# Second mixing of a two-block transformer kernel: two z or gate rows between the two heads of each delta pair

## The chip, the cores and the metric

The kernel runs as one program on one core of a Trainium2 chip. The metric is the device time of one execution in microseconds (us), lower being better; medians over runs are compared. The engines are PE (matrix multiply), DVE (vector), ACT (activation functions), POOL and SP; the last two issue only DMAs in the part of the kernel that matters here. Each engine runs its own list of instructions in order, and semaphores make one wait for another.

## The reference

Two transformer blocks in a row on a sequence of 512 tokens of width 1024. The change lies in the second block, in its "mixing", where one input projection feeds a latent attention branch and a gated delta-rule branch:

```python
h = modulate(x, g_mix[l], sh2, sc2)
proj = h @ w_in[l]
q_lat, kv_lat, k_pe, gq, gk, gv, ga, gb, gz, gates = jnp.split(proj, split_at, axis=-1)
y_mla = mla_branch(q_lat, kv_lat, k_pe, ...) @ w_o_mla[l]
y_gdn = gated_deltanet_branch(jnp.concatenate([gq, gk, gv], axis=-1), ga, gb, gz, ...) @ w_o_gdn[l]
gate_mla, gate_gdn = jnp.split(jax.nn.sigmoid(gates), N_BRANCH, axis=-1)
mixed = (gate_mla * y_mla + gate_gdn * y_gdn) @ w_out[l]
```

In the delta branch each of 8 heads has q, k and v of 128 channels. They pass a causal convolution of width 4 and a silu; q and k are normed; then a lower triangular system of 64 by 64 is solved for every chunk of 64 tokens (here by doubling in six levels), before a recurrence over the eight chunks:

```python
qkv = jax.nn.silu(causal_depthwise_conv(qkv, w_conv))
q = l2norm(to_chunks(q, DK)) * (DK ** -0.5)
k = l2norm(to_chunks(k, DK))
A = jnp.where(strict, jnp.einsum('bhnid,bhnjd->bhnij', k_beta, k) * L, 0.0)
T = lax.linalg.triangular_solve(A + eye, jnp.broadcast_to(eye, A.shape), left_side=True, lower=True, unit_diagonal=True)
w = jnp.einsum('bhnij,bhnjd->bhnid', T, k_beta * jnp.exp(decay)[..., None])
u = jnp.einsum('bhnij,bhnje->bhnie', T, v * beta[..., None])
attn_intra = jnp.einsum('bhnid,bhnjd->bhnij', q, k) * L
```

## The kernel before

Stages follow each other on every engine. The one that matters is called `delta`. In it the projection `h @ w_in` is made row by row: a "row" is a block of 128 output channels for all 512 tokens. On PE a row is 24 matmuls (`pe_three`, L237 to L239; `mix2h_Hh` and `mix2h_Hl` are the high and low parts of the input, `Wh` and `Wl` those of the weights). There are 57 rows, in the order of the list `ROWS`: 24 rows "qkv" (head, and c = 1 for k, 0 for q, 2 for v), 2 rows "kl", 6 "ql", 1 "kp", 8 "z" and 16 "g". Row 0 is made before the stage. Row n lands in one of two PSUM banks.

What is done with a row depends on its kind. A qkv row is convolved on DVE (`conv_dve`, four instructions, L2393 and L2396), then silu and, for k and q, a square on ACT; its norm follows in the next two rows (`sum_at`: four small matmul pairs on PE at L2333, a root on ACT, a reciprocal and a diagonal matrix on DVE at L2417 and L2419; `bc_at`: one broadcast matmul at L2321 and the scaling on DVE at L2410). A z or g row costs ACT one silu or sigmoid into the small ring `SPL` (L2384), and POOL one DMA from it to DRAM (`rows_pool`); it costs DVE nothing. For each row ACT also makes `Wh` (L217) and DVE makes `Wl` (L229) of the next row's weights.

Into the rows the eight heads' own work is woven. `row_steps` counts passes n = 0, 1, 2, ...; all three engines follow the same count. A pass does on each engine first the row's part, then one step of each live head, the older head first (and on DVE and ACT last the convolution, or the silu or spill, of row n). At most `NCX` = 2 heads live at once, and a head may start only when its v row is behind:

```python
if todo and at_row["qkv", todo[0], 2] < n and len(live) < NCX:
    live.append(make_head(todo.pop(0)))
live = [g for g in live if next(g, "end") != "end"]
```

A head that starts in pass s does its step j in pass s + j, and the next one may come in pass s + 16. The steps that matter below (`head_pe`, `head_act`, `head_dve`; names are those of the semaphores' keys):

- Step 0: PE `ha` (L2470); DVE two additions (L2581, L2583); ACT exponentials (L2533 to L2541).
- Step 1: PE `hkk`, 16 matmuls (L2477, L2478). It waits for the norm of the head's q.
- Step 2: PE `hkt` and `hvt` (both L171), which wait for DVE's `hla` (L2589) and `han` (L2600) of the same pass.
- Step 3: PE `hyi` (L171), which waits for `hkd` on ACT (L2549), and that for `hkb` on DVE (L2605).
- Steps 4, 6, 8, 10, 12: PE `hm1` (L2505) and, from 6 on, `hxt` (L171); ACT copies the results out (L2562, L2565).
- Steps 5, 7, 9, 11, 13: PE `hm2` (L2516); DVE waits for it and subtracts (`hy`, L2617); in steps 3 to 11 DVE then masks for the next level (`ham`, L2613).
- Step 14: PE `hw` and `hu` (L2522, L2525), each copied out by ACT (L2569, L2571).

After the last row (56) PE has passes 57 and 58 without a row, then six short products `keys_pe` (L246) in passes 59 to 64, then what is left of the heads. The next stage, `state` (its first matmul is L2861), needs all heads.

Of the kernel before, what the change touches and what calls it, by code (L numbers as in the profile page):

```python
# [96 lines left out]
def build(nc, a, out, upto="end"):  # L97
# [10 lines left out]
    def slot(name):  # L108
        m = Marks(sem(name), 16)
        dmas.append(m)  # L110
        return m
# [45 lines left out]
    def ps(b, k=1):  # L157
        return ps_t[:, b, :] if k == 1 else ps_t[:, b:b + k, :].rearrange("p b t -> p (b t)")
# [22 lines left out]
    def weight(name, blk, n, kind):  # L181

        i = len(tiles)
        tiles.append((name, blk, n, kind))
        if kind == "split":
            split_of[i] = len(split_of)
        return i
# [22 lines left out]
    def w_hi(e, i):  # L210

        s = split_of[i]
        tile_of[s] = i
        w_landed(e, i)
        if s >= NS:
            PE.wait_ge(e, ("w", tile_of[s - NS]))
        A.then_inc(e.activation(w_parts(i)[0], w_raw(i), ACT.Copy), ("w_hi", i))  # L217
# [267 lines left out]
    class Early:  # L485
# [60 lines left out]
        def rows_act(self, e, norm):  # L546
            PE.wait_ge(e, (norm.tag, "rstd"))
            A.then_inc(e.activation(self.rb, norm.bank, ACT.Copy), (norm.tag, "rows"))
# [1352 lines left out]
    class FeedForward:  # L1901
# [192 lines left out]
        def x(self, e, nb):  # L2094
# [39 lines left out]
    NSP = 3  # L2134
    SPL = PH.t("spl", NSP * 512, k=NSP)
# [26 lines left out]
    spl_out = [slot(f"spl_out{i}") for i in range(NSP)]  # L2162
# [15 lines left out]
    PAIRS = [[("qkv", h, c) for h in (2 * i, 2 * i + 1) for c in (1, 0, 2)] for i in range(4)]  # L2178
    OTHER = [("kl", n, 0) for n in range(2)] + [("ql", n, 0) for n in range(6)] + [("kp", 0, 0)] \
        + [("z", n, 0) for n in range(8)] + [("g", n, 0) for n in (*range(8, 16), *range(8))]  # L2180
    ROWS = PAIRS[0] + OTHER[0:5] + PAIRS[1] + OTHER[5:13] + PAIRS[2] + OTHER[13:21] + PAIRS[3] + OTHER[21:33]
    at_row = {key: n for n, key in enumerate(ROWS)}
    spill = {key: n for n, key in enumerate(k for k in OTHER if k[0] not in ("kl", "kp"))}
    NLD = len(spill)
    LD = nc.dram_tensor("rows_dram", [NLD, 128, 512], F32, kind="Internal").ap()
    t_row = [weight("w_in_qkv", 3 * n + c, 1024, "split") if kind == "qkv" else weight("w_in_" + kind, n, 1024, "split")
             for kind, n, c in ROWS]
    t_uk = [weight("w_ukv_k", nb, 256, "plain") for nb in range(8)]
# [37 lines left out]
    def decay_act(e):  # L2226
        PE.wait_ge(e, "tcv")
        V.wait_ge(e, "tcv")
        pv = ps(4).rearrange("p (b s h) -> p b s h", b=4, s=16)
        A.then_inc(e.activation(tcv[:, :, 2, :], pv[:, :, 0, :], ACT.Exp))  # L2230
        A.then_inc(e.activation(tcv[:, :, 3, :], pv[:, :, 2, :], ACT.Exp), "tcv")
# [51 lines left out]
    def part(h, c):  # L2283
        return (QD, KDt, Ut)[c][:, h, :]
# [15 lines left out]

    NROW = len(ROWS)
    LAT = {"k": ("kl", 2), "q": ("ql", 6)}
# [6 lines left out]
    def rows_pe(e):  # L2309
        for n in range(NROW + 2):  # L2310
            if n < NROW:
                if n >= 2:
                    (V if ROWS[n - 2][0] == "qkv" else A).wait_ge(e, ("row_out", n - 2))
                if n:
# [27 lines left out]
    def rows_act(e):  # L2342
        for n in range(NROW + 2):
            if 1 < n < NROW - 1:
                w_hi(e, t_row[n + 1])
            if n == 2:
                decay_act(e)
            if n in sum_at:
                m = sum_at[n]
                r = R4[:, 4 * (m % 3):4 * (m % 3) + 4]  # L2350
                if m >= 3:
                    V.wait_ge(e, ("ndg", m - 3))
                PE.wait_ge(e, ("nsum", m))
                A.then_inc(e.activation(r, ps(6 + m % 2)[:, 0:4], ACT.Sqrt, bias=eps1), ("nr2", m))
            if n in LSUM:
                lat_root_act(e, LSUM[n])
            yield
            if n < NROW:
                kind, h, c = ROWS[n]
                if kind == "qkv":  # L2360
                    cv = part(h, c)
                    V.wait_ge(e, ("row_out", n))
                    A.then_inc(e.activation(cv, cv, ACT.Silu), ("silu", h, c))
                    if c != 2:
                        m = norm_of[n]
                        A.wait_ge(e, ("silu", h, c))
                        if c == 0:
                            PE.wait_ge(e, ("nsum", m - 1))
                        A.then_inc(e.activation(AN[:, h, :], cv, ACT.Square), ("nsq", m))
                elif kind in ("kl", "kp"):  # L2370
                    PE.wait_ge(e, ("row", n))
                    if kind == "kl":
                        lat_square_act(e, "k", h, ps(n % 2))
                    else:
                        PE.wait_ge(e, ("k", "lsum"))
                    A.then_inc(e.activation(KL[:, h, :] if kind == "kl" else KP, ps(n % 2), ACT.Copy), ("row_out", n))
                else:
                    s = spill[ROWS[n]]
                    PE.wait_ge(e, ("row", n))
                    if kind == "ql":  # L2380
                        lat_square_act(e, "q", h, ps(n % 2))
                    if s >= NSP:
                        spl_out[s % NSP].wait_ge(e, ("spl", s - NSP))
                    A.then_inc(e.activation(SPL[:, s % NSP, :], ps(n % 2),  # L2384
                                            {"z": ACT.Silu, "g": ACT.Sigmoid}.get(kind, ACT.Copy)), ("row_out", n))
            yield
# [43 lines left out]
            yield  # L2430

    def rows_pool(e):
        for s, key in enumerate(spill):
            A.wait_ge(e, ("row_out", at_row[key]))
            spl_out[s % NSP].then_inc(e.dma_start(LD[s], SPL[:, s % NSP, :]), ("spl", s))

    def spilled(e):
        for s in range(NLD - NSP, NLD):
            spl_out[s % NSP].wait_ge(e, ("spl", s))
# [184 lines left out]
    def delta_act(e):  # L2624
        x_out.wait_ge(e, "x")
        row_steps(chain(rows_act(e), keys_act(e)), lambda h: head_act(e, h))
# [6 lines left out]
    def lat_square_act(e, s, n, o):  # L2633

        if n > 1:
            V.wait_ge(e, (s, "lsq", n - 1))
        A.then_inc(e.activation(LSQ if n else LACC[s], o, ACT.Square), (s, "lsq", n))
# [20 lines left out]
    def lat_root_act(e, s):  # L2658
        PE.wait_ge(e, (s, "lsum"))
        A.then_inc(e.activation(LR[s], ps(6)[:, 0:4], ACT.Sqrt, bias=eps1, scale=1.0 / (128 * LAT[s][1])), (s, "lroot"))  # L2660
# [572 lines left out]
    def gpsimd(e):  # L3233
        for tag, stage in (("ada1", ada1_pool), ("swa", mix1_pool), ("wout1", wout1_pool), ("query", query_pool),
                           ("gates", gates_pool), ("dense", dense_pool), ("fin", None), ("ffn1", ff1.pool), ("mix2", None),
                           ("delta", rows_pool), ("state", state_pool), ("heads", br1.pool),
                           ("b2", b2_pool), ("wout2", None), ("ffn2", None)):
            if tag in on and stage:
                stage(e)
            G.mark(("end", tag))  # L3240
# [199 lines left out]
```

## Time and profile before

| what | value |
|---|---|
| median of 3 runs | 3385.17 us (3382.62 to 3386.49) |
| span of the profiled execution, first to last instruction | 3377.5 us |
| PE busy in that span | 3226.2 us, 96% |
| stage `delta` from row 1 on | 2054.0 us to the start of `state` at 2623.4 us |
| mean granted PE clock over the whole span | 0.978 |

The profiled execution gives its span, 3377.5 us; no other time of its own is recorded, and the runs' median lies 7.7 us above it. "Busy" of PE is the time in which matmuls are under way. The granted clock is a share of full speed. A row of the kind "L171 ... [2.42 <-DVE gdnh_c L2589]" says that the engine stood idle for 2.42 us before this instruction and that DVE's instruction at line 2589 released it.

### The profile page before, as it was taken

To read this page: it belongs to the slowest core of one execution; us is meant where nothing else is said; L and a number is where in the kernel's file an instruction comes from. 1 tells how busy PE (TensorE), PEld (TensorE's weight loads), DVE (VectorE), ACT (ScalarE), POOL (GpSimd) and SP (SyncE) were. 2 spreads that over 40 slices of the span, in tenths; PEclk is the share of its full clock that TensorE was granted. 3 is DMA by queue.
4 is the path that set the end of the run, shared out by engine and by line. 5 is a ranking of instruction groups with operands and counts; after the bars stand their busy time and mean duration, and the time that the engine had idled before them with its cause. 6 is when DMAs were issued, how large, how long until landed. Compare 5 with 4: busy or idle time off the path is not lost.

```text
span 3377.5 us, 40568 instructions
## 1 busy us (share of the span) xinstructions
PE 3226.2 (96%) x16035; PEld 2671.0 (79%) x16035; DVE 2063.3 (61%) x3549; ACT 1330.8 (39%) x2340; POOL 621.1 (18%) x588
## 2 busy tenths in 40 slices
PE   8999999999999999999799997899998999999998
PEld 5764899998888888888688885687787667778887
DVE  5766887876888888888765525455443445443333
ACT  3131238983444444444422225454444124232322
POOL 0001349971222222222200000000000000000000
PEclk9999999999999999999999998899999999999999
DMA  7326244569999999998255522121221222223222
GB/s 259 125 82 222 90 137 164 201 236 349 333 332 331 331 337 327 337 328 307 80 181 183 175 88 94 53 75 62 92 80 39 70 91 72 94 81 99 95 95 80
DMA packets 190062, 574.48 MB, mean 170 GB/s; under 512 B 16305, under 2 KB 81969, under 8 KB 171569
## 3 DMA queue, kind: packets, MB, share of 16 engines
q1 hardware_dynamic: 152000, 368.06, 32.0%
q0 software_dynamic: 37872, 203.84, 16.8%
q8 instruction: 127, 2.08, 0.3%
q14 instruction: 63, 0.51, 0.0%
HBM read 523.99 MB, written 47.84 MB: 169 GB/s over the span
## 4 chain that ended last, share of the span: by engine, by line
PE 85%; DVE 8%; ACT 4%; DMA 2%; issue 1%; POOL 1%; SPq 0%; DVEq 0%; ACTq 0%; POOLq 0%
PE ps L237 11%; PE ps L238 11%; PE ps L239 11%; PE ps L1774 5%; PE ps L1773 5%; PE ps L1772 5%; PE ps L1524 4%; PE ps L1526 4%; PE ps L1525 4%; PE ps L246 4%; PE ps L744 2%; PE ps L171 1%; PE ps L1650 1%; PE ps L747 1%; DMA hidden_dram<-peerg_HS 1%; PE ps L2516 1%
## 5 line engine op out<-in xcount | busy, mean ns | idle before, releaser
L229 DVE TENSOR_TENSOR Wl<-W,Wh 128x1024 fp32r<-128x1024 f32 (+1 forms) x336 | 408.8, 1217 | 660.0 <-ACT Wh L217 659.8
L217 ACT ACTIVATE Wh<-W 128x1024 fp32r<-128x1024 f32 x362 | 377.3, 1043 | 540.7 <-PE ps L239 505.3
L1524 PE MATMUL ps<-peer_Hh,Wh 128*128 128x384 f32 x1024 | 347.8, 340 | 3.0 <-DVE Wl L229 1.4
L1526 PE MATMUL ps<-peer_Hh,Wl 128*128 128x384 f32 x1024 | 344.1, 336 | 0.0
L1525 PE MATMUL ps<-peer_Hl,Wh 128*128 128x384 f32 x1024 | 343.6, 336 | 0.0
L1737 POOL DMA_INDIRECT peerv_UV<-peer_uv,peer_EX x128 | 209.6, 1637 | 638.5 <-DVE peer_Y L1811 583.4
L1772 PE MATMUL ps<-peerv_VH,peer_HTh 128*128 128x512 f32 x768 | 300.8, 392 | 11.1 <-DVE peer_HTl L1838 11.1
L1774 PE MATMUL ps<-peerv_VH,peer_HTl 128*128 128x512 f32 x768 | 301.8, 393 | 0.0
L1773 PE MATMUL ps<-peerv_VL,peer_HTh 128*128 128x512 f32 x768 | 301.5, 393 | 0.0
L237 PE MATMUL ps<-f_Hh,Wh 128*128 128x512 f32 x656 | 257.1, 392 | 5.7 <-DVE Wl L229 5.7
L238 PE MATMUL ps<-f_Hl,Wh 128*128 128x512 f32 x656 | 256.3, 391 | 0.0
L239 PE MATMUL ps<-f_Hh,Wl 128*128 128x512 f32 x656 | 256.3, 391 | 0.0
L237 PE MATMUL ps<-mix2h_Hh,Wh 128*128 128x512 f32 x512 | 212.3, 415 | 12.6 <-DVE Wl L229 6.3
L238 PE MATMUL ps<-mix2h_Hl,Wh 128*128 128x512 f32 x512 | 206.4, 403 | 0.0
L239 PE MATMUL ps<-mix2h_Hh,Wl 128*128 128x512 f32 x512 | 206.3, 403 | 0.0
L1524 PEld LDWEIGHTS ps<-peer_Hh,Wh 128*128 128x128 f32 x1024 | 193.0, 188 | 8.5 <-ACT peerg_HS L1539 2.7
L1525 PEld LDWEIGHTS ps<-peer_Hl,Wh 128*128 128x128 f32 x1024 | 193.0, 189 | 2.8
L1526 PEld LDWEIGHTS ps<-peer_Hh,Wl 128*128 128x128 f32 x1024 | 192.7, 188 | 0.0
L1702 DVE TENSOR_TENSOR peerv_VL<-peerv_VR,peerv_VH 128x1024 fp32r<-128x1024 f32 x128 | 160.1, 1251 | 47.9 <-ACT peerv_VH L1698 47.2
L1772 PEld LDWEIGHTS ps<-peerv_VH,peer_HTh 128*128 128x128 f32 x768 | 145.1, 189 | 43.7 <-DVE peer_HTl L1838 13.0
L1774 PEld LDWEIGHTS ps<-peerv_VH,peer_HTl 128*128 128x128 f32 x768 | 144.8, 189 | 30.6
L1773 PEld LDWEIGHTS ps<-peerv_VL,peer_HTh 128*128 128x128 f32 x768 | 145.0, 189 | 27.5
(545 smaller groups left out, 6550.2 us busy)
## 6 DMA issues: line engine op xcount, KB each, us to landing
W<-peer_u SPq DMA_DIRECT2D x128, 512.0 KB, 6.8
peerv_VR<-peer_v SPq DMA_DIRECT2D x128, 512.0 KB, 5.2
gates_dram<-peerg_GB SPq DMA_DIRECT2D x12, 2048.0 KB, 7.3
peerv_GR<-gates_dram SPq DMA_DIRECT2D x32, 768.0 KB, 8.2
f_AW<-w_ada POOLq DMA_DIRECT2D x48, 512.0 KB, 4.4
W<-w_gate SPq DMA_DIRECT2D x44, 512.0 KB, 3.3
W<-w_up SPq DMA_DIRECT2D x44, 512.0 KB, 3.4
swa_AW<-w_ada POOLq DMA_DIRECT2D x32, 512.0 KB, 4.5
```

The source lines that it names most:

```text
L217: A.then_inc(e.activation(w_parts(i)[0], w_raw(i), ACT.Copy), ("w_hi", i))
L229: (G if i in lo_on_pool else V).then_inc(e.tensor_tensor(lo, w_raw(i), hi.bitcast(F32), SUB), ("w", i))
L237: e.matmul(o[0:m, :], hi[:, j, :], rhs[0][:, k, :], start=k == 0, stop=False)
L238: e.matmul(o[0:m, :], hi[:, j, :], rhs[1][:, k, :], start=False, stop=False)
L239: ins = e.matmul(o[0:m, :], lo[:, j, :], rhs[0][:, k, :], start=False, stop=k == nk - 1)
L1524: e.matmul(o, hi[:, k, :], H2[0][:, k, 0:TD], start=k == 0, stop=False)
L1525: e.matmul(o, hi[:, k, :], H2[1][:, k, 0:TD], start=False, stop=False)
L1526: ins = e.matmul(o, lo[:, k, :], H2[0][:, k, 0:TD], start=False, stop=k == 7)
L1737: uv_in[k % NUV].then_inc(e.indirect_dma_start(UV[:, k % NUV, :], None, a["peer_uv"], bass.IndirectOffsetOnAxis(ap=EX[:, k:k + 1], axis=0) ...
L1772: e.matmul(o, HTh[:, s, sl], VH[:, s, d], start=n == 0, stop=False)
L1773: e.matmul(o, HTh[:, s, sl], VL[:, s, d], start=False, stop=False)
L1774: ins = e.matmul(o, HTl[:, s, sl], VH[:, s, d], start=False, stop=n == 127)
```

## The change

The list `ROWS` is put in another order. Within each pair of heads, two z or g rows now stand between the three rows of the first head and the three of the second; these rows are taken from the runs behind the pairs, which shrink, so that later rows keep almost their place. The number and kind of rows stay. Because z and g rows now come in another order than in DRAM, the ring `SPL` gets its own numbering, `ring`, while the place in DRAM stays that of `spill`.

```diff
-    ROWS = PAIRS[0] + OTHER[0:5] + PAIRS[1] + OTHER[5:13] + PAIRS[2] + OTHER[13:21] + PAIRS[3] + OTHER[21:33]
+    KLS, QLS, KPS, ZS, GS_ = OTHER[0:2], OTHER[2:8], OTHER[8:9], OTHER[9:17], OTHER[17:33]
+
+    def apart(i, between):
+        return PAIRS[i][0:3] + between + PAIRS[i][3:6]
+
+    ROWS = apart(0, ZS[0:2]) + KLS + QLS[0:3] + apart(1, ZS[2:4]) + QLS[3:6] + KPS + ZS[4:5] + apart(2, ZS[5:7]) \
+        + ZS[7:8] + GS_[0:5] + apart(3, GS_[5:7]) + GS_[7:16]
     at_row = {key: n for n, key in enumerate(ROWS)}
     spill = {key: n for n, key in enumerate(k for k in OTHER if k[0] not in ("kl", "kp"))}
+    ring = {key: n for n, key in enumerate(k for k in ROWS if k in spill)}
...
-                    s = spill[ROWS[n]]
+                    s = ring[ROWS[n]]
...
     def rows_pool(e):
-        for s, key in enumerate(spill):
+        for key, s in ring.items():
             A.wait_ge(e, ("row_out", at_row[key]))
-            spl_out[s % NSP].then_inc(e.dma_start(LD[s], SPL[:, s % NSP, :]), ("spl", s))
+            spl_out[s % NSP].then_inc(e.dma_start(LD[spill[key]], SPL[:, s % NSP, :]), ("spl", s))
```

The rule of `row_steps` turns the order into the passes in which heads start:

| head | 0 | 1 | 2 | 3 | 4 | 5 | 6 | 7 |
|---|---|---|---|---|---|---|---|---|
| place of its v row, before | 2 | 5 | 13 | 16 | 27 | 30 | 41 | 44 |
| place of its v row, now | 2 | 7 | 15 | 20 | 28 | 33 | 42 | 47 |
| starts in pass, before | 3 | 6 | 19 | 22 | 35 | 38 | 51 | 54 |
| starts in pass, now | 3 | 8 | 19 | 24 | 35 | 40 | 51 | 56 |

What this does to an engine's list is seen at two places. The first is DVE in pass 53, where head 6 does its step 2 (`gdnh_c0_*` are the tiles of an even head, `gdnh_c1_*` those of an odd one). Before:

```order
L229 TENSOR_TENSOR Wl<-W,Wh 128x1024 [waits act_done] x2
L2589 SCALAR_TENSOR_TENSOR gdnh_c0_1<-ps,gdn_tc,gdnh_c0_1 128x128 [waits pe_done]
L2589 SCALAR_TENSOR_TENSOR gdnh_c0_1<-ps,gdn_tc,gdnh_c0_1 128x128 x3
L2593 TENSOR_TENSOR gdnh_c0_2<-gdnh_c0_1,consts_sb 128x512 [waits dve_done]
L2595 TENSOR_TENSOR gdnh_c0_3<-consts_sb,gdnh_c0_2 128x512 [waits dve_done]
L2598 TENSOR_TENSOR gdnq_QD<-gdnq_QD,gdnh_c0_0 128x512
L2600 TENSOR_TENSOR gdnc_AN<-ps,gdnc_AN 128x512
```

The same place with the change (lines are eight further down):

```order
L229 TENSOR_TENSOR Wl<-W,Wh 128x1024 [waits act_done] x2
L2625 TENSOR_TENSOR gdnh_c1_4<-gdnh_c1_4,ps 128x512 [waits pe_done]
L2597 SCALAR_TENSOR_TENSOR gdnh_c0_1<-ps,gdn_tc,gdnh_c0_1 128x128 x4
L2601 TENSOR_TENSOR gdnh_c0_2<-gdnh_c0_1,consts_sb 128x512 [waits dve_done]
L2603 TENSOR_TENSOR gdnh_c0_3<-consts_sb,gdnh_c0_2 128x512 [waits dve_done]
L2606 TENSOR_TENSOR gdnq_QD<-gdnq_QD,gdnh_c0_0 128x512
L2608 TENSOR_TENSOR gdnc_AN<-ps,gdnc_AN 128x512
```

Head 5's step 13, `hy` of the last level, which waits for a product of PE in this pass, now stands in front of head 6's step 2. It is the same in pass 21 (heads 1 and 2) and 37 (heads 3 and 4). Before, the odd head had nothing left to do in these passes.

The second place is DVE in passes 4 and 5, where head 0 does its steps 1 and 2. Before:

```order
L2396 SCALAR_TENSOR_TENSOR gdnq_QD<-ps,vecs_sb,gdnq_QD 128x509 [waits dve_done]
L229 TENSOR_TENSOR Wl<-W,Wh 128x1024 [waits act_done]
L2410 SCALAR_TENSOR_TENSOR gdnc_KD<-gdnc_KD,ps 128x512 [waits pe_done]
L2417 RECIPROCAL small<-small 128x4 [waits act_done]
L2419 TENSOR_TENSOR DG<-consts_sb,small 128x512 [waits dve_done]
L2589 SCALAR_TENSOR_TENSOR gdnh_c0_1<-ps,gdn_tc,gdnh_c0_1 128x128 x4
```

And now:

```order
L2418 SCALAR_TENSOR_TENSOR gdnq_QD<-gdnq_QD,ps 128x512 [waits pe_done]
L229 TENSOR_TENSOR Wl<-W,Wh 128x1024 [waits act_done]
L2597 SCALAR_TENSOR_TENSOR gdnh_c0_1<-ps,gdn_tc,gdnh_c0_1 128x128 [waits pe_done]
L2597 SCALAR_TENSOR_TENSOR gdnh_c0_1<-ps,gdn_tc,gdnh_c0_1 128x128 x3
L2601 TENSOR_TENSOR gdnh_c0_2<-gdnh_c0_1,consts_sb 128x512 [waits dve_done]
```

The convolution of head 1's q row and the norm work of head 1's k row no longer stand between head 0's steps; rows 3 and 4 are z rows now.

The third place is ACT in pass 54, head 6's step 3. Before:

```order
L217 ACTIVATE Wh<-W 128x1024 [waits w_in0]
L2549 ACTIVATE gdnc_KD<-ps,gdn_tc 128x128 [waits dve_done,pe_done]
L2549 ACTIVATE gdnc_KD<-ps,gdn_tc 128x128 x3
L2553 ACTIVATE X<-ps,gdn_tc 128x128 [waits pe_done]
L2553 ACTIVATE X<-ps,gdn_tc 128x128 x3
```

And now:

```order
L217 ACTIVATE Wh<-W 128x1024 [waits w_in0]
L2577 ACTIVATE mix2_YG<-ps 128x512 [waits pe_done]
L2579 ACTIVATE X<-ps 128x512 [waits pe_done]
L2557 ACTIVATE gdnc_KD<-ps,gdn_tc 128x128 [waits dve_done]
L2557 ACTIVATE gdnc_KD<-ps,gdn_tc 128x128 x3
```

The two copies of head 5's step 14, which wait for PE's `hw` and `hu` behind this pass's row, have come in front of `hkd`; before, they lay one or more passes earlier.

## Rows read from the trace of the kernel before

**Rows 1.** The page: the span, and PE's busy time in it

```profile
span 3377.5 us, 40568 instructions
PE 3226.2 (96%) x16035; PEld 2671.0 (79%) x16035; DVE 2063.3 (61%) x3549; ACT 1330.8 (39%) x2340; POOL 621.1 (18%) x588
```

**Rows 2.** Windows: rows 1 to 56; behind them. Length, busy times, clock, DMA

```profile
2054.00:2572.00 518.00, 474.76 (x2446) 393.78 (x2447) 258.55 (x387) 254.58 (x421) 15.69 (x29) 0.94 0.22 75
2572.00:2623.00 51.00, 40.20 (x251) 32.85 (x249) 18.55 (x33) 17.87 (x36) 2.06 (x3) 0.90 0.09 26
```

**Rows 3.** PE's waits from 2054 to 2624: total, times, longest

```profile
PE ps L171 <- DVE gdnh_c L2589: 13.7, 6, 2.5
PE ps L171 <- ACT gdnc_KD L2549: 11.4, 5, 3.3
PE ps L171 <- DVE gdnc_AN L2600: 11.3, 6, 2.0
```

**Rows 4.** Timeline of PE, passes 24 and 25: hm2, hkt, hvt; hyi

```profile
2292.62 1.05 PE L2516 MATMUL ps<-gdnh_c,gdnh_c 128*128 128x128 f32 x8
2296.09 0.87 PE L171 MATMUL ps<-consts_sb,gdnc_KD 128*128 128x128 f32 x4 [2.42 <-DVE gdnh_c L2589]
2298.75 1.12 PE L171 MATMUL ps<-consts_sb,X 128*128 128x128 f32 x4 [1.79 <-DVE gdnc_AN L2600]
...
2310.07 0.66 PE L171 MATMUL ps<-consts_sb,gdnh_c 128*128 128x128 f32 x4 [1.77 <-ACT gdnc_KD L2549]
```

**Rows 5.** Timeline of DVE, pass 24: hy, ham, hla, the last is han

```profile
2293.71 0.69 DVE L2617 TENSOR_TENSOR gdnh_c<-gdnh_c,ps 128x512 f32<-128x512 f32 x1 [4.87 <-PE ps L2516]
2294.32 0.68 DVE L2613 TENSOR_TENSOR gdnh_c<-gdnh_c,consts_sb 128x512 f32<-128x512 f32 x1
2294.92 1.12 DVE L2589 SCALAR_TENSOR_TENSOR gdnh_c<-ps,gdn_tc,gdnh_c 128x128 f32<-128x128 f32 x4
...
2298.01 0.68 DVE L2600 TENSOR_TENSOR gdnc_AN<-ps,gdnc_AN 128x512 f32<-128x512 f32 x1
```

**Rows 6.** Timeline of ACT, pass 25: the older head's copy, hkd

```profile
2308.39 0.59 ACT L2565 ACTIVATE gdnh_c<-ps 128x512 f32<-128x512 f32 x1
2308.87 1.14 ACT L2549 ACTIVATE gdnc_KD<-ps,gdn_tc 128x128 f32<-128x128 f32 x4
```

**Rows 7.** Timeline of PE, passes 53 and 54: hkt, hvt; hyi

```profile
2549.17 0.60 PE L171 MATMUL ps<-consts_sb,gdnc_KD 128*128 128x128 f32 x4
2549.60 0.60 PE L171 MATMUL ps<-consts_sb,X 128*128 128x128 f32 x4
...
2555.50 0.60 PE L171 MATMUL ps<-consts_sb,gdnh_c 128*128 128x128 f32 x4
```

**Rows 8.** Windows over rows 25, 42 and 54 alone, columns as in rows 2

```profile
2299.50:2306.80 7.30, 7.30 (x26) 5.89 (x25) 1.61 (x5) 0.00 (x0) 0.00 (x0) 0.74 0.22 72
2452.50:2459.70 7.20, 7.20 (x27) 5.76 (x26) 5.13 (x7) 3.46 (x6) 0.00 (x0) 0.76 0.00 0
2549.90:2555.40 5.50, 5.50 (x27) 4.59 (x26) 2.50 (x5) 2.87 (x10) 0.54 (x1) 1.00 0.19 73
```

**Rows 9.** Timeline of PE, head 0 in passes 4, 5, 5 and 6

```profile
2094.78 1.05 PE L2333 MATMUL ps<-consts_sb,gdnc_AN 128*128 128x1 f32 x8 [0.74 <-ACT gdnc_AN L2369]
...
2110.68 0.66 PE L171 MATMUL ps<-consts_sb,gdnc_KD 128*128 128x128 f32 x4 [2.33 <-DVE gdnh_c L2589]
2113.34 1.12 PE L171 MATMUL ps<-consts_sb,X 128*128 128x128 f32 x4 [2.00 <-DVE gdnc_AN L2600]
...
2126.21 1.11 PE L171 MATMUL ps<-consts_sb,gdnh_c 128*128 128x128 f32 x4 [3.29 <-ACT gdnc_KD L2549]
```

**Rows 10.** Timeline of PE, head 7 alone at the stage's end

```profile
2612.49 1.06 PE L2516 MATMUL ps<-gdnh_c,gdnh_c 128*128 128x128 f32 x8
2614.93 1.16 PE L2505 MATMUL ps<-gdnh_c,gdnh_c 128*128 128x128 f32 x8 [1.38 <-DVE gdnh_c L2613]
...
2617.36 1.13 PE L2516 MATMUL ps<-gdnh_c,gdnh_c 128*128 128x128 f32 x8 [0.83 <-ACT gdnh_c L2565]
```

More of the change, by code:

```diff
@@ L2180, in build @@
         + [("z", n, 0) for n in range(8)] + [("g", n, 0) for n in (*range(8, 16), *range(8))]
-    ROWS = PAIRS[0] + OTHER[0:5] + PAIRS[1] + OTHER[5:13] + PAIRS[2] + OTHER[13:21] + PAIRS[3] + OTHER[21:33]
+    KLS, QLS, KPS, ZS, GS_ = OTHER[0:2], OTHER[2:8], OTHER[8:9], OTHER[9:17], OTHER[17:33]
[3 more added lines that the diff above has]
+        + ZS[7:8] + GS_[0:5] + apart(3, GS_[5:7]) + GS_[7:16]
+    assert sorted(ROWS) == sorted(sum(PAIRS, []) + OTHER)
     at_row = {key: n for n, key in enumerate(ROWS)}
     spill = {key: n for n, key in enumerate(k for k in OTHER if k[0] not in ("kl", "kp"))}
+    ring = {key: n for n, key in enumerate(k for k in ROWS if k in spill)}
     NLD = len(spill)
```

## Prediction

> **What bounds the kernel now.** I read the page first. PE is busy in 3226.2 of 3377.5 us [rows 1]; what can move is its idle time and the time in which its clock is low. The change touches only the stage with the 57 rows, so I took windows of that stretch next. From row 1 to the end of row 56 PE is busy in 474.8 of 518 us, so it idles for 43 us; behind the rows it idles for 10.8 of 51 us. DVE and ACT are half idle there (259 and 255 us) and DMA is at 0.22 [rows 2], so no engine but PE is full, and PE's idle time comes from chains between engines, not from load. The waits of PE in that stretch name the chains: `hkt` for DVE's `hla` 13.7 us in 6 waits, `hvt` for `han` 11.3 us in 6, `hyi` for ACT's `hkd` 11.4 us in 5 [rows 3]. All three belong to steps 2 and 3 of a head. Six waits for eight heads: the timeline shows that head 4 and head 6 have none. In pass 53 head 6's `hkt` and `hvt` follow the row at once, and so does its `hyi` in pass 54 [rows 7].
>
> **Why some heads wait.** Pass 24 has a z row behind it and no convolution in front; yet head 3 waits 2.42 and 1.79 us [rows 4]. DVE shows why: it stood 4.87 us until PE's `hm2` of head 2, which is in its step 5, then made `hy` and `ham`, and only then `hla` (at 2294.92) and `han` (at 2298.01) [rows 5]. DVE takes the older head first and waits in that step for a product that PE makes behind this pass's row, while PE comes to the younger head's `hkt` right behind that product. So the rule is: when a head does step 2 while an older one does an odd step from 5 to 13, PE waits for the whole DVE chain. In pass 25 the like happens on ACT: its copy of head 2's `hxt` (2308.39) comes before `hkd` (2308.87), and PE waits 1.77 us [rows 4, 6]. Head 6 has no older head at work, and DVE did `hla` under the row.
>
> **What the change does to these meetings.** Before, an odd head meets the even one in its step 5 (offset 3), now in its step 7 (offset 5). Both are odd: the wait stays. But the next even head now meets the odd one before it in that one's step 13 instead of its empty step 15, and its `hyi` stands behind that one's `hw` and `hu`. That gives waits to heads 4 and 6, which had none. I price it head by head; PE's own work and the count of instructions stay the same.
>
> *Heads 4 and 6* (passes 37, 38 and 53, 54). Step 13 has `hy` but no `ham`, so `hkt` waits 2.42 less 0.6, 1.8 us; `hvt` waits 1.79 to 2.0, I take 1.9; `hyi` behind two ACT copies instead of one with its last matmul just before: 1.8 [rows 4, 6, 9]. Then the clock: row 25, behind such a wait, took 7.3 us at a granted 0.74, row 54 took 5.5 at 1.00 [rows 8]; 0.74 is a mix of the two levels 1.2 and 2.4 GHz. So each pair of waits costs 1.8 us more in the next row. Row 42, behind a `hyi` wait, took 7.2 [rows 8], but not each such wait does this, so for the second row I take 0.5 of a possible 1.7. Last, `ham` of step 11 now delays step 0's additions by 0.6, and with them ACT's weights; 0.6, from 0 to 1.2. Together 1.8 + 1.9 + 1.8 + 1.8 + 0.5 + 0.6 = 8.4 per head, 16.8 us (from 2 x 5.5 with no clock term at all to 2 x 10).
>
> *Head 2* (passes 21, 22) gets the same 7.8, but has waits already: from 13.7 and 11.3 us the five heads 0, 1, 3, 5, 7 take about 12.1 and 9.8 at the prices in [rows 4, 9], which leaves 1.6 and 1.5 for head 2, and 1.3 of clock in proportion. 7.8 - 4.4 = 3.4. Its step 0 now falls among its own pair's rows: ACT's exponentials delay the square of q, as in pass 4, where PE waited 0.74 [rows 9]; 1.0, from 0 to 2. Together +4.4.
>
> *Head 0* gains. In pass 5 there is no older head; it waits 2.33 and 2.00 because the norm of head 1's k row and the convolution stand before `hla` [rows 9]. Rows 3 and 4 are z rows now and DVE has nothing there: -4.3. The 0.74 wait in pass 4 goes: -0.7. In pass 6 `hyi` waited 3.29 [rows 9]; now the convolution of row 5, the root and the diagonal come before `hkb`: +0.7 (from 0 to 1.5). One slow row fewer: -1.7. Together -6.0 (from -9 to -4).
>
> *Heads 1, 3, 5*: offsets of the same kind, waits as before. Head 1: 0. Head 3 now has its steps 2 and 3 beside its successors' k and q rows (26, 27), so `hkb` stands behind a norm: +1.6 (0 to 3). Head 5's step 0 falls on row 40, a k row, whose square then comes late: +1.6 (0 to 3). Together +3.2.
>
> *The end.* Head 7 starts in pass 56 instead of 54. Two of its steps, one level of `hm1` and `hm2`, leave the six passes with `keys_pe` and are done alone: there PE waits 1.38 and 0.83 [rows 10], +2.2. Its `hkk` in pass 57 has no row any more that covers the two additions on DVE (0.6 to 0.7 each, as their kind in [rows 5]) and ACT's first exponential behind them; PE's `hm1` and `hxt` of head 6, 1.7 us, stand in between, so I take +1.1 (an estimate, 0 to 3). Together +3.3 (2 to 5).
>
> Sum: -6.0 + 4.4 + 16.8 + 3.2 + 3.3 = +21.7. The profiled execution gives 3377.5 + 21.7 = 3399.2 us of span; the median of the runs lies 7.7 above the span, 3385.2 + 21.7 = **3407 us**.
>
> The clock terms in this sum are worth about 5 us. The Trainium skill ("TensorE: Matmul & The Clock Gate", Part 1: The HAM clock gate) says "For modeling, the ramp penalty is <1% of a typical kernel span"; by that one would leave them out, and the sum would be +17, 3402 us. I keep them, since rows 25 and 42 have their price beside them.
>
> The DMAs of the ring are as many as before and its three places are still used in the order of the rows; POOL issues nothing else then. I price that at nothing; if a spill came late, ACT would stand with the weights behind it. DMA at 0.22 [rows 2] speaks against it.
>
> **Rivals.** What a run of this kernel can tell from no change is about 0.2%, 6.8 us.
>
> 1. *The waits come as priced*: +12 to +32, centre +21.7. Chance 0.68.
> 2. *Heavier* (0.10): late DVE and ACT work in passes 20 to 27 and 36 to 43 carries on from pass to pass, so that the upper ends hold together: -4 + 5.4 + 20 + 6 + 5 = +32, 3418 us and above, up to +42. Against it: of PE's 43 us of idle time in the passes with rows, the three chains of steps 2 and 3 make 30 (36.4 less some 6 behind row 56) [rows 2, 3]; late weights are no large part of it.
> 3. *Absorbed* (0.15): the third meeting is cheaper. Step 13's `hy` alone costs 0.6 on DVE; if DVE could do part of head 6's step 2 beside it, or PE came later, only the `hyi` waits would stay: 2 x 2.3 + 1.5 - 6 + 3.3 = +3, 3388 us. For it speaks head 0's gain of 6, which is certain in kind; against it the order of DVE, in which `hy` stands ahead of `hla`. 0.10 of this within 0.2%, 0.05 slower.
> 4. *Faster* (0.07): the mechanism is DVE's convolutions and norms, not the meeting. Then thinning the qkv rows takes from heads 1, 3, 5 and 7 what it takes from head 0: with 6.0 at head 0 and a third of it at three others, -12, 3373 us. It decides if the four later pairs of waits drop by over 5 us each more than heads 4 and 6 gain. Against it: head 3 waits 2.42 and 1.79 with no convolution before it [rows 4, 5], as much as head 0 with one.
>
> **How the numbers follow.** Slower by over 0.2%: 0.68 + 0.10 + 0.05 = 0.83; within 0.2%: 0.10; faster 0.07. The range leaves out the fast case, most of the absorbed one and the top of the heavier one: 3390 to 3420. The likeliest case alone spans 3397 to 3417.
>
> **What would show it.** Right: PE's waits for `hla` and `han` (now L2597 and L2608) come in 7 waits each, sums near 15 and 14 us; those for `hkd` (L2557) in 8, near 18; passes 37 and 53 show about 3.7 us, where there was none; pass 5 shows none; behind the last `keys_pe` two levels stand alone; rows 38 and 54 take over 7 us at a clock near 0.75. Wrong: `hkt` of heads 4 and 6 without a wait, or the waits of heads 1, 3, 5 much under 4 us, would overturn the meeting rule; a stage longer by the sum with a kernel no slower would mean that the next stage took it back.

## The result and the profile after

The changed kernel takes 3399.93 us in the median of 4 runs (3397.92 to 3407.07), the kernel before on the same chip 3384.05 us; the ratio is 1.0055 with a 95% interval of 1.0043 to 1.0067, so it is slower by 0.55%. The profiled execution has a span of 3397.6 us against 3377.5. Of these 20.1 us, 17.5 lie in the stage with the rows (from row 1's first matmul to the first of `state`: 2057.0 to 2643.9 us, before 2054.0 to 2623.4). The other 3.0 lie ahead of the stage, where nothing was changed: in the traces of this case row 1 starts anywhere from 2054.0 to 2062.0 us. The rest behind the stage is the same within 0.4 us. I therefore compare stages. A stage length comes from one profiled execution; in all the runs below it and the medians agree within 3.4 us on the distance to the kernel before. Here the medians differ by 15.9 us: the profiled execution of the kernel before was one of its faster ones.

The page of the changed kernel, and windows over rows 1 to 55, over row 56 and over what lies behind it, to be read beside [rows 1, 2], where row 56 is in the first window:

```profile
span 3397.6 us, 40563 instructions
PE 3229.9 (95%) x16035; PEld 2671.2 (79%) x16035; DVE 2063.6 (61%) x3549; ACT 1331.3 (39%) x2340; POOL 621.8 (18%) x588
...
2057.00:2577.00 520.00, 465.26 (x2401) 386.06 (x2401) 257.20 (x385) 247.93 (x405) 15.15 (x28) 0.95 0.21 74
2577.00:2582.40 5.40, 5.40 (x27) 4.46 (x26) 0.00 (x0) 2.37 (x3) 0.54 (x1) 1.00 0.12 49
2582.60:2643.00 60.40, 44.24 (x271) 33.96 (x269) 19.22 (x35) 22.24 (x47) 2.06 (x3) 0.92 0.07 22
```

The instructions are the same. In the stage PE is busy for 514.9 us, before 515.0; it idles for 54.7 us beside the rows where it was 43.2, and for 16.2 behind them where it was 10.8. PE's waits in the stage (engine and line, who released it, total us, times, longest) answer to [rows 3]:

```profile
PE ps L171 <- ACT gdnc_KD L2557: 17.2, 8, 3.7
PE ps L171 <- DVE gdnh_c L2597: 15.2, 7, 2.5
PE ps L171 <- DVE gdnc_AN L2608: 13.5, 7, 2.0
PE ps L2524 <- ACT gdnh_c L2573: 5.2, 3, 3.5
```

The waits for `hla` (L2597) went from 13.7 us in 6 to 15.2 in 7, those for `han` (L2608) from 11.3 in 6 to 13.5 in 7, those for `hkd` (L2557) from 11.4 in 5 to 17.2 in 8. The fourth row is new: `hm2` waits for ACT's copies, before 0.8 us in one.

Passes 53 and 54 are where head 6 had no wait [rows 7]. The timeline of PE there now: `hm2` of head 5, `hkt`, `hvt`; `hw` of head 5; `hyi`:

```profile
2553.54 1.05 PE L2524 MATMUL ps<-gdnh_c,gdnh_c 128*128 128x128 f32 x8
2556.41 0.66 PE L171 MATMUL ps<-consts_sb,gdnc_KD 128*128 128x128 f32 x4 [1.82 <-DVE gdnh_c L2597]
2559.06 1.12 PE L171 MATMUL ps<-consts_sb,X 128*128 128x128 f32 x4 [2.00 <-DVE gdnc_AN L2608]
...
2566.53 1.05 PE L2530 MATMUL ps<-gdnh_c,mix_YG 128*128 128x128 f32 x8
...
2570.19 0.66 PE L171 MATMUL ps<-consts_sb,gdnh_c 128*128 128x128 f32 x4 [1.72 <-ACT gdnc_KD L2557]
```

DVE in pass 53 of the same kernel:

```profile
2554.63 0.69 DVE L2625 TENSOR_TENSOR gdnh_c<-gdnh_c,ps 128x512 f32<-128x512 f32 x1 [4.40 <-PE ps L2524]
2555.24 1.12 DVE L2597 SCALAR_TENSOR_TENSOR gdnh_c<-ps,gdn_tc,gdnh_c 128x128 f32<-128x128 f32 x4
...
2558.32 0.68 DVE L2608 TENSOR_TENSOR gdnc_AN<-ps,gdnc_AN 128x512 f32<-128x512 f32 x1
```

And ACT in pass 54, the copy of `hu` and then `hkd`:

```profile
2568.51 0.60 ACT L2579 ACTIVATE X<-ps 128x512 f32<-128x512 f32 x1 [0.29 <-PE ps L2533]
2569.00 1.14 ACT L2557 ACTIVATE gdnc_KD<-ps,gdn_tc 128x128 f32<-128x128 f32 x4
```

DVE stood idle for 4.40 us with all that head 6's step 2 needs at hand, because head 5's subtraction is ahead in its list and waits for PE. PE finishes that product and then waits 1.82 and 2.00 us for what DVE could have done meanwhile. Pass 37 with head 4 shows the same 1.8 and 2.0.

Head 0's gain, in passes 5 and 6 (`hkt`, `hvt`; `hyi`), against [rows 9]:

```profile
2107.15 0.60 PE L171 MATMUL ps<-consts_sb,gdnc_KD 128*128 128x128 f32 x4
2107.59 0.60 PE L171 MATMUL ps<-consts_sb,X 128*128 128x128 f32 x4
...
2118.18 0.83 PE L171 MATMUL ps<-consts_sb,gdnh_c 128*128 128x128 f32 x4 [3.74 <-ACT gdnc_KD L2557]
```

The clock, in windows over rows 38, 54 and 55 alone:

```profile
2409.50:2416.20 6.70, 6.70 (x26) 5.49 (x25) 1.57 (x5) 0.00 (x0) 0.00 (x0) 0.81 0.22 78
2559.80:2566.50 6.70, 6.70 (x26) 5.47 (x25) 1.62 (x5) 0.00 (x0) 0.00 (x0) 0.82 0.06 20
2570.60:2576.20 5.60, 5.60 (x28) 4.61 (x27) 2.51 (x3) 2.01 (x5) 0.54 (x1) 1.00 0.21 73
```

The row behind the two waits runs at 0.81 and costs 1.1 us more than 5.6; the row behind the `hyi` wait of 1.7 us is at full clock.

### The profile page after: what moved, and what is told of

The parts are those of the page before. It is cut to its first block, busy times and chain, and to the rows that moved or that the text cites. A ratio compares the mean times of both kernels' runs of the same rounds, so it can differ in the third digit from the quotient of the medians.

```text
span 3397.6 us, 40563 instructions
## 1 busy us (share of the span) xinstructions
PE 3229.9 (95%) x16035; PEld 2671.2 (79%) x16035; DVE 2063.6 (61%) x3549; ACT 1331.3 (39%) x2340; POOL 621.8 (18%) x588
## 4 chain that ended last, share of the span: by engine, by line
PE 80%; DVE 8%; ACT 5%; DMA 3%; POOL 2%; issue 1%; SPq 0%; DVEq 0%; ACTq 0%; POOLq 0%
PE ps L237 11%; PE ps L239 11%; PE ps L238 11%; PE ps L1773 5%; PE ps L1774 5%; PE ps L1772 5%; PE ps L1524 4%; PE ps L1526 4%; PE ps L1525 4%; PE ps L744 2%; PE ps L246 2%; DMA hidden_dram<-peerg_HS 1%; PE ps L171 1%; DMA adaw_AW<-w_ada 1%; PE ps L747 1%; PE ps L2524 1%
```

## The experiments

The runs are numbered by their paragraphs. My theory: what the change costs comes from which steps of two heads fall into one pass, given that DVE and ACT serve the older head first; the order of the rows sets this only through the starts. The rival: the convolutions and norms beside the heads, that is DVE's own load. All times are compared with the kernel before on the same chip; "stage" is from row 1 to `state` in the profile (569.4 before, 586.9 with the change).

**1. The starts alone** (rows as before).

```diff
+    START = [3, 8, 19, 24, 35, 40, 51, 56]
-            if todo and at_row["qkv", todo[0], 2] < n and len(live) < NCX:
+            if todo and at_row["qkv", todo[0], 2] < n and START[todo[0]] <= n and len(live) < NCX:
```

> The rows stand in the order of the kernel before; only the passes in which heads 1, 3, 5 and 7 may start are held back by two, to 8, 24, 40 and 56, as the change has them. Theory (meetings of steps decide): all waits of the change come, and head 0's gain does not, since rows 3 and 4 are qkv rows again; waits of PE for hla and han in 8 and 8, for hkd in 8; 3384 plus 20 to 26, about 3407 us. Rival (the place of the convolutions decides): the starts alone do nothing beyond the two lone steps at the end, 3384 to 3390 us.

Measured: 3405.39 us against 3382.04, ratio 1.0067 (1.0054 to 1.0081); stage 593.3, +23.9 us. PE's waits:

```profile
PE ps L171 <- DVE gdnh_c L2591: 18.0, 8, 2.8
PE ps L171 <- ACT gdnc_KD L2551: 16.6, 8, 3.3
PE ps L171 <- DVE gdnc_AN L2602: 14.6, 8, 2.0
```

No row has moved, and the whole loss is there, and more: eight waits of each kind, since head 0 keeps its own. The 6.4 us between the two stages, 23.9 and 17.5, are what the new row order itself gives. The rival's first form, by which the starts alone would do nothing beyond the end, is out.

**2. Head 7 alone held back to pass 56** (rows as before, with the condition of run 1), to price the end.

```diff
+    START = [0, 0, 0, 0, 0, 0, 0, 56]
```

> The kernel before with head 7 alone held back to pass 56; all other heads start as before. It isolates the term of the end, which the prediction put at 3.3 us. What the changed kernel's waits behind row 56 say (15.0 us against 9.1, less 0.6 before it) is about 5.3: 3382 plus 5, 3387 us, waits of PE behind the last row near 15 us with one of 3.5 on ACT's copy. If the prediction's size was right: 3385. Rival (the end costs nothing, all of the change lies in the passes with rows): 3382.

Measured: 3389.08 us against 3382.73, ratio 1.0022 (1.0013 to 1.0031); stage 575.6, +6.3 us. PE's waits behind row 56:

```profile
PE ps L2518 <- ACT gdnh_c L2567: 5.2, 3, 3.5
PE ps L2507 <- DVE gdnh_c L2615: 2.8, 2, 1.4
```

The end costs 6.3, not 3.3. In the changed kernel the same wait of 3.5 stands in pass 58. ACT of the changed kernel, timeline behind row 56: head 7's exponentials, a table load, the spill of row 56, and only then the copies of head 6; and PE's `hm2` that waits for them:

```profile
2586.93 1.26 ACT L2545 ACTIVATE gdnh_c<-gdnh_c,gdn_tc 128x128 f32<-128x128 f32 x4
2588.10 1.26 ACT L2549 ACTIVATE gdnc_AN<-gdnc_AN,gdn_nds 128x128 f32<-128x128 f32 x4
2589.38 1.28 ACT L2392 ACT_TABLE_LOAD   x1
2590.68 0.60 ACT L2392 ACTIVATE gdnh_spl<-ps 128x512 f32<-128x512 f32 x1
2591.17 0.59 ACT L2570 ACTIVATE gdnh_c<-ps 128x512 f32<-128x512 f32 x1
2591.65 0.60 ACT L2573 ACTIVATE gdnh_c<-ps 128x512 f32<-128x512 f32 x1
...
2592.40 1.52 PE L2524 MATMUL ps<-gdnh_c,gdnh_c 128*128 128x128 f32 x8 [3.51 <-ACT gdnh_c L2573]
```

In the passes with rows PE has a row's 5.6 us to cover step 0's work on ACT; here it has none.

**3. An offset of 4** (rows as before, with the condition of run 1).

```diff
+    START = [3, 7, 19, 23, 35, 39, 51, 55]
```

> Rows in the order of the kernel before; the odd heads may start one pass later than before (7, 23, 39, 55), an offset of 4. Theory: an odd head's step 2 now meets the older one's step 6, which asks nothing of DVE, so the waits for hla and han of heads 1, 3, 5 and 7 go (about -17.7 us); its step 3 meets step 7, so hyi waits some 4 us instead of 1.7 to 2.3 (+8); the next even head meets step 14 in its step 2 and nothing in step 3, no wait; one lone step more at the end, +1 to +3. Sum about -7, 3377 us (3370 to 3384). Rival (a later start costs by how much later it is): between before and the change, 3388 to 3396 us.

Measured: 3382.67 us against 3382.04, ratio 1.0 (0.9991 to 1.0009); stage 569.1. The time is inside the expected range, but the gain of 7 us did not come.

```profile
PE ps L171 <- ACT gdnc_KD L2551: 19.4, 5, 4.3
PE ps L171 <- DVE gdnc_AN L2602: 9.9, 5, 2.0
...
PE ps L171 <- DVE gdnh_c L2591: 4.1, 3, 2.3
```

The waits for `hla` fell from 13.7 to 4.1 as the theory says, and `hyi` paid 3.9 to 4.3 at each odd head. But five waits for `han` stayed: that of head 0 in pass 5, which was there before; one in pass 57, where no row stands between `hkk` and step 2; and three that stand behind norm work on DVE, in pass 21 (latent sum) and in passes 9 (latent sum) and 41 (norm of a q row), where `hla` too waits 0.9. Those three are no meeting. The rival has a share after all: without a meeting, a norm beside step 2 costs PE 3 us.

**4. One row between the heads of each pair** instead of two; the same starts as run 3.

```diff
-    ROWS = apart(0, ZS[0:2]) + KLS + QLS[0:3] + apart(1, ZS[2:4]) + QLS[3:6] + KPS + ZS[4:5] + apart(2, ZS[5:7]) \
-        + ZS[7:8] + GS_[0:5] + apart(3, GS_[5:7]) + GS_[7:16]
+    ROWS = apart(0, ZS[0:1]) + KLS + QLS[0:3] + ZS[1:2] + apart(1, ZS[2:3]) + QLS[3:6] + KPS + ZS[3:5] + apart(2, ZS[5:6]) \
+        + ZS[6:8] + GS_[0:5] + apart(3, GS_[5:6]) + GS_[6:16]
```

> One z or g row between the heads of a pair instead of two, the other rows moved to keep the later pairs' places. The starts are 3, 7, 19, 23, 35, 39, 51, 55. Theory: as the offset of 4 with the old rows, and part of head 0's gain besides (its convolution in pass 4 goes, the norm in pass 5 stays): 3368 to 3382 us, about 3375. Rival (thinning is what it takes, more rows between are better or worse in proportion): half way between before and the change, about 3392 us.

Measured: 3369.81 us against 3382.04, ratio 0.9966 (0.9954 to 0.9978); stage 556.1. The size fits, one reason given for it does not: head 0 still waits 2.3 and 2.0 in pass 5, since row 4 is a k row there and its norm stands ahead of `hla`. What is gone against run 3 are the waits in pass 9 and pass 21, three waits for `han` being left of five. Against the change itself, with its two rows, this is 31 us of stage: one row fewer turns a loss into a gain.

**5. One row between in pair 0 alone**, pairs 1 to 3 together; the starts of runs 3 and 4. The edit takes the place of the two added lines of run 4.

```diff
+    ROWS = apart(0, ZS[0:1]) + KLS + QLS[0:3] + PAIRS[1] + QLS[3:6] + KPS + ZS[1:5] + PAIRS[2] + ZS[5:8] + GS_[0:5] + PAIRS[3] \
+        + GS_[5:16]
```

> One row between the heads of pair 0 alone; the six rows of pairs 1, 2 and 3 stand together as before, one place later for pair 1. Starts as with one row everywhere (3, 7, 19, 23, 35, 39, 51, 55). Theory: what differs between the two runs of offset 4 (12 us) is where single norm sums and the latent sums fall, not the spread of convolutions: two of the passes with a head's step 2 (9 and 21) come free of them here too; 3370 to 3378 us. Rival (spreading each pair's convolutions is what gains): near the offset of 4 with the old rows, 3380 to 3384.

Measured: 3372.68 us against 3380.77, ratio 0.9976 (0.9965 to 0.9988); stage 562.9, half way between runs 3 and 4 (569.1 and 556.1). The waits for `han` are the same three of 6.0 us as in run 4, those for `hkd` 22.4 us in 6 against 19.4 in 5. So of the 13.0 us of stage between runs 3 and 4, 6.2 are where single sums fall and 6.8 the spread of the later pairs; by the medians, each against its own kernel before, it is 8.7 and 4.1. Both readings had a part, and these runs do not fix the shares more closely.

**6. DVE serves the younger head first in its step 2** (the changed kernel, rows as changed).

```diff
-    def row_steps(rows, make_head):
+    def row_steps(rows, make_head, first=()):
...
             if todo and at_row["qkv", todo[0], 2] < n and len(live) < NCX:
-                live.append(make_head(todo.pop(0)))
-            live = [g for g in live if next(g, "end") != "end"]
+                live.append([make_head(todo.pop(0)), -1])
+            for g in live:
+                g[1] += 1
+            over = [g for g in sorted(live, key=lambda g: g[1] not in first) if next(g[0], "end") == "end"]
+            live = [g for g in live if g not in over]
...
-        row_steps(rows_dve(e), lambda h: head_dve(e, h))
+        row_steps(rows_dve(e), lambda h: head_dve(e, h), (2,))
```

The second entry of `g` counts the head's steps; a head whose step is in `first` is served ahead of the other.

> The changed kernel; on DVE alone the head that is in its step 2 comes before the older head in that pass (every other pass as it was). Theory: hla and han no longer stand behind a subtraction that waits for PE; the waits of PE for them, 15.2 and 13.5 us in 7 each, fall under 8 us together, while those for hkd stay near 17 us; with the slow rows behind them -20 to -30, 3370 to 3380 us. Rival (DVE is late by its own load, convolutions and norms): the waits only move to the older head's next product, less than 8 us are gained.

Measured: 3364.32 us against 3382.04, ratio 0.9955 (0.9941 to 0.9968); stage 555.1, 31.8 us less than with the change and 14.3 less than before. The time lies below the expected 3370 to 3380; the waits came as expected.

```profile
PE ps L171 <- ACT gdnc_KD L2560: 18.0, 8, 3.7
...
PE ps L171 <- DVE gdnc_AN L2611: 4.0, 2, 2.0
...
PE ps L171 <- DVE gdnh_c L2600: 2.3, 2, 1.3
```

This is the direct test: the same instructions and starts, one order exchanged, and 28.7 us of waits for `hla` and `han` become 6.3. The four that remain lie in passes 21 and 42, beside norm work.

**7. The same, and ACT serves the younger head first in its step 3.**

```diff
-        row_steps(chain(rows_act(e), keys_act(e)), lambda h: head_act(e, h))
+        row_steps(chain(rows_act(e), keys_act(e)), lambda h: head_act(e, h), (3,))
```

> The changed kernel; as the run before, DVE takes the head in its step 2 first, and besides ACT takes the head in its step 3 first. Theory: hkd no longer stands behind ACT's copies of the older head; the waits of PE for hkd fall from 17 to about 8 us (head 0's 3.7 and those that hang on norms stay), -10 to -16 with the slow rows against the run with DVE alone: 3364 minus 12, 3352 us (3346 to 3358). Rival: ACT's place is not what holds hyi, but hkb on DVE: no change against 3364.

Measured: 3362.35 us against 3380.77, ratio 0.9942 (0.9926 to 0.9959); stage 549.2, 5.9 us less than run 6. The medians show less of it: 18.4 us below the kernel before, where run 6 was 17.7 below, with intervals that overlap (the profiled execution of run 6 is 3 us shorter behind the stage than the others). That this step shortened the time is thus seen in the waits and the stage of one trace each, not in the runs' times.

```profile
PE ps L171 <- ACT gdnc_KD L2560: 11.5, 5, 3.7
```

The waits in passes 22, 38 and 54, the ones that the change had made, are gone. Of the expected 10 to 16 us at least half did not come: the waits of heads 0, 1, 3 and 5 (3.8, 2.3, 3.1 and 2.0 us) stayed as they were in run 6, so they do not hang on ACT's copies; `hkb` or a norm ahead of it is what is left.

**8. Both orders on the kernel before** (the edits of runs 6 and 7).

> The kernel before with the same two orders of heads. Theory: the change costs 18 us only through the meetings, so with both orders free of them the two row orders come near each other; what is left between them is head 0 (6 to 7 us for the change) against the two lone steps at the end (5 us against it): 3352 plus or minus 4. Rival (the row order itself costs): before stays about 18 us ahead of the changed one, near 3335.

Measured: 3360.23 us against 3380.77, ratio 0.9933 (0.9916 to 0.995); stage 547.3. The absolute time was missed by 8 us for the reason given under run 7, but the question was the distance: 17.5 us of stage between the two row orders have become 1.9 (549.2 and 547.3). The medians of runs 7 and 8 are 2.1 us apart. With the meetings made harmless, two rows between or none hardly matters.

**9. One row between (the rows of run 4), younger first on DVE in steps 2 and 3, on ACT in step 3.**

```diff
+        row_steps(rows_dve(e), lambda h: head_dve(e, h), (2, 3))
+        row_steps(chain(rows_act(e), keys_act(e)), lambda h: head_act(e, h), (3,))
```

> One row between the heads of a pair, and younger first: DVE in steps 2 and 3, ACT in step 3. Theory: at offset 4 the odd heads wait 3.9 us in step 3 because DVE's subtraction and mask for the older head, which wait for PE, come before hkb; with hkb first, four waits of 3.9 us shrink to under 1: -14 to -22 against 3370, 3352 us (3346 to 3358). Rival: hy of the younger head, which now waits for hyi before the older head is served, gives the time back: 3365 to 3372.

Measured: 3362.77 us against 3380.77, ratio 0.9945 (0.9929 to 0.9962); stage 549.1, 7.0 less than run 4, half of what I expected. The waits for `hkd` went from 19.4 us in 5 to 9.9 in 4. Together with runs 7 and 8 this puts three row orders within 1.9 us of stage; what is left in all of them are head 0's and head 5's norm waits, the start of the stage and the end. Runs 6 to 9 beat both kernels; among 7, 8 and 9 there is no difference that these runs can tell.

## Why the prediction was right

The time was 3399.93 us where 3407 was forecast, inside the range. The kernel is slower, as forecast; by how much, 15.9 us between the medians and 17.5 of stage, is less than the 21.7 of the sum.

*The rule of meetings* held to the count: 7, 7 and 8 waits were forecast for `hla`, `han` and `hkd` with sums near 15, 14 and 18 us; 15.2, 13.5 and 17.2 came. Runs 1 and 6 show that it is the cause and not a companion.

*Heads 4 and 6*: 8.4 each was forecast. Waits of 1.8, 2.0 and 1.7 came (1.8, 1.9 and 1.8 forecast); the slow row cost 1.1 instead of 1.8 and there was no second one; late weights cost 0.2 instead of 0.6. Together 6.8 each. One of the signs named did not come: rows 38 and 54 took 6.7 us at 0.81 and 0.82, not over 7 near 0.75. But this count leaves out the short products of the same passes, some of which also ran at the low clock. From the start of row 36 to that of row 39, and from 52 to 55, the changed kernel takes 31.7 us where 22.5 stood before; about 1.0 of these 9.2 is the odd head's work that has moved there, net of what has left (an estimate from passes at full clock). That makes 8.2 each: the clock cost about what I had put down for it, in other places.

*Head 2*: +4.4 forecast. Its waits are 0.9, 1.8, 2.0 and 1.7 where there were 3.1, and the slow row 1.6 for 1.4; +3.5, or +3.3 counted with the short products in the same way.

*Head 0*: -6.0 forecast, -6.5 from the waits and rows of passes 4 to 7. With the short products, which before ran at the low clock behind these waits, the gain is larger. From the start of row 1 to that of row 8 the changed kernel takes 71.3 us where 84.9 stood before; about 3.8 of these 13.6 is work that has moved behind row 8 (again an estimate from passes at full clock), which leaves -9.8. Run 1, with the same starts and the old rows, takes 80.5, of which 0.9 is such work: 8.3 for the row order alone up to there. Its 6.4 for the whole stage is a balance of this gain and some loss later. The 0.74 wait of pass 4 did not vanish, it moved: PE waited 2.8 instead of 1.8 for the next thing, the norm of q.

*Heads 1, 3, 5*: 0, +1.6, +1.6 forecast; 0, -0.2, +1.3 came. Head 5's 1.7 us in pass 41 is as described. Head 3's `hyi` waited 2.3 where it waited 1.8 before, a third of the 1.6, and it lost the 0.6 for late weights that it had before row 24.

*The end*: +3.3 forecast, +6.3 measured by itself in run 2. The lone level is there, its 1.38 and 0.83 a second time. What I missed is ACT behind `hkk`: I priced the first exponential, and the copies of the older head also stand behind the rest of them, a table load and the last spill. The step's range, 2 to 5, was too short.

In the order of the heads and then the end, the parts give -9.8 + 0 + 3.3 - 0.2 + 8.2 + 1.3 + 8.2 + 6.3 = +17.3 for a stage that grew by 17.5. The sum of 21.7 was 4 too high. Its largest errors are head 0's gain, 4 too small, and the end, 3 too cheap; they have opposite signs, so that part of the closeness is luck. Head 3 was 1.8 too dear and head 2 about 1. The sentence on the clock rule of the Trainium skill ("TensorE: Matmul & The Clock Gate", Part 1) gave +17, and its sum fits better here. By the sum's own terms it gives nearer +18: the clock terms are 2.3 at each of heads 4 and 6, 1.0 net at head 2 and -1.7 at head 0, 3.9 together. But not because slow rows cost nothing: behind such waits each costs 1.1 to 2.4 us in the trace. The change made new ones (rows 38, 54) and took away others (rows 5 and 6 in pair 0, the second one at head 5), so that over the rows it is even within 1 us.

The 7.7 us that I put between the span and the runs' median is not a fixed part around the span: the changed kernel's profiled execution took 3399.42 us for a span of 3397.6, which is 1.8. The rest was that the profiled execution of the kernel before was a fast one.

Rival 2 (heavier) had one of its signs, the end above its bound, and not the others. Rival 3 (absorbed) is out by the waits of passes 37 and 53 and by run 1. Rival 4 (DVE's load) is out as the main cause by runs 1 and 6, but runs 3 and 6 show that it has its own passes, 9 and 41 in the one, 21 and 42 in the other, of about 3 us each. The prediction's head 0 was such a case; besides it I had norm work in the sum only at heads 3 and 5, and there as a delay of 1.6 us.

## What to carry to other kernels

Where two chains are woven into one another pass by pass on engines that work in order, list for each pass which step of one meets which step of the other, and look for a step that waits for a product of this very pass standing ahead of one that has all it needs. Putting the ready one first costs no instruction and on DVE alone was worth 32 us of stage here. On the kernel before, doing so on both engines gained 22.1 us of stage, the best order of rows tried 13.3. A change of spacing should be judged by the offsets it makes (3 to 5 kept the bad meeting and added another; 4 avoided both and paid with longer waits for `hyi`), and a start that moves toward the end of a stage by the work that used to cover it, on every engine.

## What the runs showed of the hardware

How long a slow row is after the same kind of wait varies: after `hkt` and `hvt` waits of 1.8 and 2.0 us, row 38 took 6.7 us at a clock of 0.81 and row 22 took 7.2 at 0.76; behind `hyi` waits of 1.7 rows 39 and 55 took 5.6, at 1.00. A single wait of 3.7 us (pass 6) gave a row of 7.1. An ACT table load shows 1.28 us, and the next activation starts 0.02 us behind its end (2589.38 plus 1.28, then 2590.68); the Trainium skill ("ScalarE: Activation LUTs", What ACT_TABLE_LOAD costs) agrees on the 1.28 and adds about as much again for a drain, of which nothing is seen here.
